# Moving the transfers between K's start and the second norm of a diffusion layer on 8 cores

## The reference, cut to what matters

```
mod = silu(c) @ w_ada + b_ada                   # six rows: shift1 scale1 gate1 shift2 scale2 gate2
h   = rmsnorm(x, g1) * (1 + scale1) + shift1     # also for the context tokens, with c_ctx
q, k, v, u = split(h @ w_in)                     # 1536 | 512 | 512 | 512
q, k = rope(rmsnorm(q per head)), rope(rmsnorm(k per head))
attn = softmax(q k^T / sqrt(128)) v              # 12 query heads on 4 key heads, keys: 256 context + 2048 latent
four = Re(fft2(u over positions and group channels)) @ w_fourier    # 4 groups of 128 channels
x   = x + gate1 * (concat(attn, four) @ w_out)
h2  = rmsnorm(x, g2) * (1 + scale2) + shift2
x   = x + gate2 * (relu(h2 @ w1)^2 @ w2)         # 8192 wide
out = rmsnorm(x, final_g)
```

## Time and profile before

| | |
|---|---|
| time, median of 3 executions | 1690.61 us (1689.73 to 1691.33) |
| the profiled execution | 1697.91 us |
| its slowest core's span | 1696.4 us (the cores: 1680.1 to 1696.4) |
| PE busy, share of the span | 1551.4 us, 91% |
| DVE | 841.5 us, 50% |
| ACT | 578.6 us, 34% |
| POOL | 414.9 us, 24% |
| transfers that POOL issues (software_dynamic) | 142.65 MB, 52.7% of the 16 DMA engines' span |
| transfers that SP issues (hardware_dynamic) | 39.31 MB, 6.9% |

### The profile page before, as it was taken

One profiled execution on the slowest core, in us unless ns is written; L12 is line 12 of the kernel. 1 busy time (PEld: TensorE's weight loads), 2 busy tenths in 40 slices (PEclk: granted clock), 3 DMA queues, 4 the chain that ended last, 5 costly groups with the idle time before them and its releaser, 6 DMA issues.

```text
span 1696.4 us, 27654 instructions; the slowest of 8 cores (1680.1 to 1696.4 us)
## 1 busy us (share of the span) xinstructions
PE 1551.4 (91%) x8936; PEld 782.8 (46%) x9084; DVE 841.5 (50%) x1229; ACT 578.6 (34%) x1000; POOL 414.9 (24%) x236
## 2 busy tenths in 40 slices
PE   0279989997899899989999999999999999999997
PEld 0145434444677676434444444444444444444443
DVE  0067687775688576466233333333333333333346
ACT  1055254334789797005311111111111111111145
POOL 1000045432001000040404412442144314441320
PEclk9999999999999999999999999999999999999999
DMA  9999997757375964955335254434534353525524
GB/s 172 186 270 240 166 135 116 118 76 111 67 133 119 169 117 76 230 70 82 54 52 97 51 100 72 77 63 88 93 58 81 69 100 51 99 50 100 89 76 159
DMA packets 90401, 183.73 MB, mean 108 GB/s; under 512 B 3858, under 2 KB 62994, under 8 KB 86802
## 3 DMA queue, kind: packets, MB, share of 16 engines
q0 software_dynamic: 78640, 142.65, 52.7%
q1 hardware_dynamic: 11620, 39.31, 6.9%
HBM read 316.20 MB, written 8.39 MB: 191 GB/s over the span
## 4 chain that ended last, share of the span: by engine, by line
PE 76%; DMA 15%; DVE 5%; issue 2%; ACT 2%; POOL 0%; DVEq 0%; ACTq 0%; POOLq 0%; SPq 0%
PE psum L284 75%; DMA arena<-w_ada 9%; DMA arena<-x_own 2%; DVE arena L291 2%; DMA arena<-dft_alt 1%; DMA arena<-w_in 1%; DMA arena<-w_out 1%; PE psum L288 1%; DVE arena L432 1%; DVE arena L644 1%; ACT arena L392 0%; ACT arena L1056 0%; ACT arena L429 0%; DVE arena L816 0%; DVE arena L1053 0%
## 5 line engine op out<-in xcount | busy, mean ns | idle before, releaser
L284 PE MATMUL psum<-arena 128*128 128x512 bf16 (+3 forms) x8256 | 1520.6, 346 | 118.2 <-DMA arena<-w_ada 78.1
L284 PEld LDWEIGHTS psum<-arena 128*128 128x128 bf16 (+1 forms) x8404 | 742.6, 99 | 866.1 <-issue 161.7
L291 DVE TENSOR_TENSOR arena<-psum,arena 128x512 f32<-128x512 f32 (+2 forms) x594 | 403.2, 715 | 617.0 <-PE psum L284 574.5
L291 POOL TENSOR_TENSOR arena<-arena 128x2048 bf16<-128x2048 bf16 (+1 forms) x102 | 308.2, 3035 | 329.4 <-DMA arena<-w 221.5
L1135 ACT ACTIVATE arena<-psum 128x512 f32<-128x512 f32 x128 | 75.3, 588 | 661.9 <-PE psum L284 661.9
L890 ACT ACTIVATE arena<-psum 128x768 bf16<-128x768 f32 x288 | 223.6, 810 | 49.0 <-PE psum L284 42.3
L281 POOL DMA_DIRECT2D arena<-w_ada x48 | 34.4, 718 | 401.1 <-PE psum L284 161.0
L291 DVE TENSOR_TENSOR arena<-arena 128x256 f32<-128x256 f32 (+3 forms) x159 | 113.8, 717 | 33.1 <-DMA arena<-w 14.5
L816 DVE SCALAR_TENSOR_TENSOR arena<-arena 128x1024 f32<-128x1024 bf16 x94 | 117.3, 1275 | 8.9 <-DMA arena<-w_ada 8.4
L392 ACT ACTIVATE arena<-arena 128x2048 bf16<-128x2048 f32 x26 | 49.7, 1910 | 205.7 <-DVE arena L291 103.0
L281 POOL DMA_DIRECT2D arena<-w x24 | 25.4, 1058 | 267.9 <-PE psum L284 191.9
(11 more groups left out here) (52 smaller groups left out, 279.4 us busy)
## 6 DMA issues: line engine op xcount, KB each, us to landing
arena<-w_ada POOLq DMA_DIRECT2D x48, 1024.0 KB, 15.6
arena<-w POOLq DMA_DIRECT2D x24, 2048.0 KB, 15.5
arena<-x_own SPq DMA_DIRECT2D x16, 1024.0 KB, 19.0
arena<-w_in POOLq DMA_DIRECT2D x7, 2048.0 KB, 20.7
arena<-w POOLq DMA_DIRECT2D x8, 1536.0 KB, 11.6
arena<-x_oth SPq DMA_DIRECT2D x8, 1024.0 KB, 12.4
out<-arena SPq DMA_DIRECT2D x16, 512.0 KB, 3.4
arena<-w_out POOLq DMA_DIRECT2D x3, 2048.0 KB, 29.4
```

Of the source, the lines that this page charges most:

```text
L284: S.add('pe', lambda e, o_=out, l=lhsT, r=rhs, a=start, b=stop, kw=kw: e.matmul(o_, lhsT=l, rhs=r, start=a, stop=b, **kw), reads=reads, wr ...
L291: S.add(eng, lambda e, o_=out, a=in0, b=in1, op=op: e.tensor_tensor(out=o_, in0=a, in1=b, op=op), reads=reads, writes=writes)
```

## The change

Nothing of the arithmetic changes. In the order of the stages:

- V: of shift1's first three pieces only the first is issued at once. The second is issued at tile 1 and reads the key of the buffer that then holds tile 4, the third at tile 2 with that of tile 6. So they wait until these tiles have landed.
- K: the steps of scale2's generator begin at unit 4, not 2; two of them fall into Q.
- Q: the second and third column block of w_in are loaded after unit 0 of the block before instead of unit 1. `make_gs` and `v_rows` come at unit 7 instead of 5. The row `dft_alt` is loaded at unit 3 of block 1 into the area of the used-up rotary tables, no longer at the start of attention into the area of the normed tokens. The last unit's `qk_two` stands before `v_proj` and the first refills.
- Attention: `prefetch_wo` is cut into four transfers, 2, 30, 55 and 70 steps after the end of `fourier`.
- Output projection: the four multiplies of `load_w2(0)` are put behind `load_wo(3)`.
- Second norm: for the last three tiles `norm2_flip` is put before `norm2_stats`.

```
-        for p in range(3):
-            load_ada(0, p, ADA1, 'ada')
+        load_ada(0, 0, ADA1, 'ada')
...
+            if t in (1, 2):
+                load_ada(0, t, ADA1, 'ada', after=['xt%d' % (t * 2 - 2)])
...
-            if t >= 2:
+            if t >= 4:
                 next(g4)
...
-                if cb == 0 and t == 1:
+                if cb == 0 and t == 0:
                     wslot[1] = load_wb(w_in[:, 512:1024])
...
-                if cb == 1 and t == 1:
+                if cb == 1 and t == 0:
                     wslot[2] = load_wb(w_in[:, 1024:1536])
+                if cb == 1 and t == 3:
+                    S.alias('alt', ['ropr%d' % i for i in range(4)])
+                    dma('pool', AV(P0 + 14 * KB, 2 * KB, BF16)[0:1, :], alt_d[:, :], 'alt', writes=['alt'])
...
-                if cb == 0 and t == 5:
+                if cb == 0 and t == 7:
                     make_gs(2, 4, 0, g2col, 'g2col')
                     v_rows()
                 if cb == 2 and t == 7:
+                    qk_two(len(QKU) - 1)
                     v_proj()
...
-        qk_two(NQK - 1)
...
-        ALT = AV(G(14), 2 * KB, BF16)[0:1, :]
+        ALT = AV(P0 + 14 * KB, 2 * KB, BF16)[0:1, :]
...
-        dma('pool', ALT, alt_d[:, :], 'alt', writes=['alt'])
...
-        def prefetch_wo():
...
+        def prefetch_wo(n):
+            if n < 2:
+                S.alias('wof%d' % n, ['ft'])
+                dma('pool', HFR[:, :, n * 512:(n + 1) * 512], w_out[n * 1024:(n + 1) * 1024, 0:512].rearrange("(k p) n -> p k n", p=128), 'wof%d' % n, writes=['wof%d' % n])
+            else:
+                t = n - 2
...
                 dma('sp', ACC[t], x_own[t * 128:(t + 1) * 128, :], 'acc%d' % t, writes=ACCK(t))
...
-                    prefetch_wo()
+                    pre = [(k + 2, 0), (k + 30, 1), (k + 55, 2), (k + 70, 3)]
+            while pre and k >= pre[0][0]:
+                prefetch_wo(pre.pop(0)[1])
...
-        def load_w2(b):
+        def load_w2(b, part=2):
             s = b % 2
+            if part == 1:
+                return gate_w2(b)
...
+            if part == 2:
+                gate_w2(b)
+
+        def gate_w2(b):
+            s = b % 2
             for j in range(4):
                 tt('dve' if b == NB - 1 and j >= 2 else 'pool', W2C[s][j], W2C[s][j], GT2, ALU.mult, ['w2s%d' % s] + ['gt5_%d' % i for i in range(4)], ['w2g%d_%d' % (s, j)])
...
                 if cb == 3:
+                    if t >= 5:
+                        norm2_flip(0, (range(0, 2), range(2, 5), range(5, 8))[t - 5])
                     n2[t] = norm2_stats(t)
                     if 1 <= t <= 4:
                         norm2_x(t - 1, n2[t - 1])
-                    if t >= 5:
-                        norm2_flip(0, (range(0, 2), range(2, 5), range(5, 8))[t - 5])
...
-                load_w2(0)
+                load_w2(0, 0)
             if cb == 1:
                 load_wo(3)
+                load_w2(0, 1)
```

More of the change, by code:

```diff
@@ L778, in build_program @@
         GT2 = AV(T0 + 12 * KB, 8 * KB)
-        for k in (['mixT_%d' % t for t in range(8)] + ['on0', 'on1', 'wcs', 'alt', 'onesf']
+        for k in (['mixT_%d' % t for t in range(8)] + ['on0', 'on1', 'wcs', 'onesf']
                   + ['pt%d' % i for i in range(4)] + ['abt%d_%d' % (i, j) for i in range(2) for j in range(2)]):
@@ L924, in build_program @@
         g_ada, g_four = ada_rest(), fourier()
-        def prefetch_wo():
[L926 to L931, removed]
+        def prefetch_wo(n):
[4 more added lines that the diff above has]
+                t = n - 2
+                OLDP = ['pq%d_%d' % (v, c) for v in range(2) for c in range(4)] + ['ext', 'ada2', 'shb', 'rope3'] + ['ropr%d' % i for i in range(4)] + ['alt']
                 for kk in ACCK(t):
@@ L934, in prefetch_wo @@
                 dma('sp', ACC[t], x_own[t * 128:(t + 1) * 128, :], 'acc%d' % t, writes=ACCK(t))
+        pre = []
         flips = []
@@ L969, in build_program @@
                 if four_st[0] == 'end':
-                    prefetch_wo()
+                    pre = [(k + 2, 0), (k + 30, 1), (k + 55, 2), (k + 70, 3)]
+            while pre and k >= pre[0][0]:
+                prefetch_wo(pre.pop(0)[1])
             if pr == NPAIR - 1:
                 norm_O(ui)
-        assert four_st[0] == 'end' and not flips
+        assert four_st[0] == 'end' and not flips and not pre
         for _ in g_ada:
```

## The result

The changed kernel takes **1674.35 us** (median of 3 executions, 1673.55 to 1675.04) against 1690.61 us: a ratio of 0.9896, with an interval of 0.9868 to 0.9924. The forecast was 1667, range 1659 to 1679: right in sign and within the range, 7.3 us too low.

The account below looks back on a forecast made before the run. The slowest core bounds the time, its busiest engine PE losing time in waits before 815 us. Core 7's terms sum to 26.2, 1693.6 to 1667.4; 1.5 around the span and half of 4.5 carried over give 1667 us, range 1659 to 1679.

Parts of the forecast that it names:

- the failed step: Output projection: fourth w_out block issued before POOL's gate multiplies; 0 for core 7, bounds 0 and a gain of 4.2 us.
- V: V stage, two shift pieces held: PE reaches the late w_ada piece up to 5.8 us sooner, waits that much longer; 0.
- a longer wait than 2.78 us on w_ada at the end of V: End of V: sign that the forecast is right, PE's wait for the fifth shift piece growing beyond 2.78 us.
- the rival that I had set apart: V stage: held pieces block SP's tile loads, making the kernel slower than before, 1694 us; chance 0.06.
- SP waiting on w_ada past tile 8: V stage: sign that the forecast is wrong, SP's tile loads held up by shift pieces past tile 8.
- the rival's 17.8: V stage, tile 8: loss in us if a held piece takes 37.8 us, beyond the 20.0 that cost nothing.
- K and Q: K's fourth unit to the idle time ahead of attention: core 7 falls from 164.15 to 161.04 us, gain 3.1.
- qk_two: Start of attention: V row's copy on DVE now stands behind the last unit's rotary work; loss 0.7 us.
- dft_alt and prefetch: Attention: dft_alt's 8.58 us wait and 2.6 of clock go, 11.2; w_out and x prefetch in four steps, 8.3.
- Second norm: Second norm: 2.57 us wait for ACT's copy and 2.5 of clock at stake, 5.1; 0.8 left, gain 4.3 us.
- The sum: Core 7, all terms: 0 + 3.1 - 0.7 + 11.2 + 8.3 + 0 + 4.3 = 26.2 us gained.

Follow-up runs that it names:

- kq_back: The changed kernel with the K and Q edits undone (scale2's steps, w_in's blocks and the V bias rows as before): ratio 0.9968 (0.9951 or 0.9953 to 0.9982).
- its version with the split multiplies: The kernel before with one edit alone, the four multiplies by gate2 put behind the fourth w_out block: ratio 1.0055 (1.0039 to 1.0071).
- the first and the third set: First: variants of where the gate2 multiplies stand, ratios 0.9890 to 1.0055. Third: other edits undone in the changed kernel, ratios 0.9966 to 0.9999, dft_alt's without ratio.

## Why the prediction was near, and the step that failed

**Output projection: the failed step.** "The multiplies start later by the time until w_out's slot is free, and have the whole fourth column block to spare", priced 0 for core 7 with bounds of 0 and a gain of 4.2. I asked whether the multiplies would be in time for their user, not whom they hinder. The move cost 7.70 us: 5.96 of wait and, by the two windows, 0.55 x 0.42 + 5 x 0.27 = 1.6 of clock. The trace of before already had adds of 3.79 us beside these multiplies, and I had not read DVE there; with them the bound would have had a loss in it. That an add would wait for all four could not be read from before.

**V: 0 came out, but not for the reason given.** The reason was that PE gets to the late piece of w_ada sooner and stays in that wait for as much longer. The sign of it, "a longer wait than 2.78 us on w_ada at the end of V", didn't show: the wait got shorter. What takes the gain back lies earlier. The held pieces block SP, the rival that I had set apart: its sign, SP waiting on w_ada past tile 8, did show, and it costs PE 3.5 to 4.8 us behind tile 8, far less than the rival's 17.8. And the clock falls behind that one wait, a term that I hadn't put in for V. That this comes to 0 is luck.

**K and Q: right.** 161 us on all cores (160.7 to 161.4), and with the edits undone three of them take 2.7 us more. **qk_two: right**, 0.75 forecast as 0.7. **dft_alt and prefetch: right together**, 18.71 of 19.5 on core 7; undone singly they cost 13.1 and 11.1 us within the set, more than the 11.2 and 8.3, so the two gains don't simply add. Core 7 gave some back: its clock was 0.50 from 565 to 570 us, though the records show no wait of PE over 0.16 us there.

```profile
565.00:570.00 5.00, 5.00 (x30) 3.99 (x30) 1.43 (x5) 1.62 (x2) 0.00 (x0) 0.50 1.04 172
```

**Second norm: right**, 928.0 against 932.9 on core 0; core 7 lost 1.6 of it to a late product on POOL in the MLP.

**The sum** was near in part by luck: the 7.70 us lost stand against 3.5 us in core 7's first two stages (-4.94 and +1.42) that the hold does not explain.

**Not settled.** In the MLP a core now and then waits for a weight block, up to 12.44 us in a profiled execution (core 3 of kq_back); in the kernel before and its version with the split multiplies none of 16 cores does. And in the first and the third set attention takes 9 to 10 us longer on one half of the chip than on the other in the kernels that have it as changed. I made no run for either.

## What to carry to other kernels

When work is moved on an off-path engine, ask what it locks out there, not only whether it is in time: read the durations of the other engines' instructions beside it, for one that is longer than its like. Don't let POOL run a row of SBUF work straight behind a transfer's issue while DVE adds two SBUF operands; make each piece wait for a tile's result instead, which costs nothing here. When an edit puts one wait in the place of several, read the clock behind it too: here one of 3.52 us was followed by 0.50, three of 1.57 to 2.11 us by 1.00. Of a stage in one profiled execution, ask how far it varies before a difference is put down to an edit: V's 144.50 us didn't come back in the other kernels without the hold.

## What the hardware showed

DVE's add with two SBUF operands doesn't run beside POOL's multiply (3.79 us instead of 0.69); DVE's multiply with one operand in PSUM does (0.68 to 0.69 us there as elsewhere). The Trainium skill ("SBUF — State Buffer", "Who interferes with whom") says so: an instruction of DVE with two SBUF inputs contends with a GpSimd instruction that reads SBUF, and the page's summary adds that the second to issue is blocked until the first finishes. The trace agrees where an add is held 3.8 us by one multiply. It goes further in the changed kernel: 14.67 us, four multiplies, and 17.64 us when the add began during the issue of the transfer ahead of them. Three microseconds of idle time on POOL between issue and multiplies end this; why, how little would do, and whether other POOL work than a transfer's issue right ahead of the row would shut DVE out as well, is not shown.
